# GpSimd takes the weights' remainder in two instructions of 512 columns instead of one of 1024

## The reference, cut to what matters

```python
sc = jnp.einsum('thpd,hpkd->thpk', q, subkeys)        # scores against 2 x 128 keys, 8 heads
s1, i1 = lax.top_k(sc[:, :, 0], 16)
s2, i2 = lax.top_k(sc[:, :, 1], 16)
cand = (s1[..., :, None] + s2[..., None, :])...       # 16 x 16 sums
best, pos = lax.top_k(cand, 16)                       # the experts of each token and head
gate = jax.nn.softmax(best)
act = gelu(einsum('phkd,pd->phk', u_tab[idx], t)) * gate
out = einsum('phk,phkd->pd', act, v_tab[idx])
```

## Time and profile before

| | |
|---|---|
| time, median of 3 runs | 3680.57 us (3678.1 to 3683.18) |
| the profiled execution's own time | 3682.65 us |
| its span, first to last instruction | 3680.8 us |
| TensorE busy | 3566.2 us, 97% |
| VectorE, ScalarE, GpSimd busy | 2295.2, 1473.8, 960.2 us |
| GpSimd's 63 subtractions (L289) | 167.9 us |
| mean granted TensorE clock | 0.989 |

### The profile page before, as it was taken

One profiled execution on the slowest core, in us unless ns is written; L12 is line 12 of the kernel. 1 busy time (PEld: TensorE's weight loads), 2 busy tenths in 40 slices (PEclk: granted clock), 3 DMA queues, 4 the chain that ended last, 5 costly groups with the idle time before them and its releaser, 6 DMA issues. The chain is left out here.

```text
span 3680.8 us, 55968 instructions
## 1 busy us (share of the span) xinstructions
PE 3566.2 (97%) x22572; PEld 3258.7 (89%) x22572; DVE 2295.2 (62%) x3902; ACT 1473.8 (40%) x2191; POOL 960.2 (26%) x795
## 2 busy tenths in 40 slices
PE   8999999999999998999999999999999999999998
PEld 8988999998887688888668876899999999999998
DVE  7445465545754546555686444469988886677775
ACT  7254453223635435222475433333333443333333
POOL 4010022112401013111114000058956662111110
PEclk9999999999999999999999999999999999999999
DMA  4211233222221133222221222347869999999884
GB/s 153 70 46 59 75 115 98 92 92 86 70 70 58 52 109 120 93 97 92 80 79 49 75 93 75 96 150 260 258 197 262 294 285 338 314 308 309 306 308 137
DMA packets 293616, 544.69 MB, mean 148 GB/s; under 512 B 138288, under 2 KB 187568, under 8 KB 292976
## 3 DMA queue, kind: packets, MB, share of 16 engines
q1 hardware_dynamic: 185248, 394.34, 32.7%
q0 software_dynamic: 27648, 100.68, 8.2%
q10 hardware_dynamic: 80464, 46.10, 4.2%
HBM read 483.67 MB, written 56.62 MB: 147 GB/s over the span
## 5 line engine op out<-in xcount | busy, mean ns | idle before, releaser
L314 PE MATMUL PSM<-UX,PARTS 128*128 128x264 f32 (+3 forms) x2976 | 1017.0, 342 | 33.5 <-POOL PARTS L289 6.8
L272 ACT ACTIVATE PARTS<-RAW 128x1024 fp32r<-128x1024 f32 x612 | 645.3, 1056 | 953.0 <-PE PSM L316 486.8
L315 PE MATMUL PSM<-UX,PARTS 128*128 128x264 f32 (+3 forms) x2976 | 1001.3, 336 | 0.0
L316 PE MATMUL PSM<-UX,PARTS 128*128 128x264 f32 (+3 forms) x2976 | 1000.2, 336 | 0.0
L282 DVE TENSOR_TENSOR PARTS<-RAW,PARTS 128x1024 fp32r<-128x1024 f32 x549 | 694.2, 1270 | 487.8 <-ACT PARTS L272 487.6
L314 PEld LDWEIGHTS PSM<-UX,PARTS 128*128 128x128 f32 x2976 | 562.6, 189 | 91.0 <-issue 15.7
L315 PEld LDWEIGHTS PSM<-UX,PARTS 128*128 128x128 f32 x2976 | 562.5, 189 | 35.3 <-issue 1.9
L316 PEld LDWEIGHTS PSM<-UX,PARTS 128*128 128x128 f32 x2976 | 561.4, 189 | 35.0
L3102 PE MATMUL PSM<-AC,PARTS 128*128 128x416 f32 x1024 | 359.9, 351 | 2.2 <-DVE AC L3399 2.2
L3103 PE MATMUL PSM<-AC,PARTS 128*128 128x416 f32 x1024 | 359.1, 351 | 0.0
L3104 PE MATMUL PSM<-AC,PARTS 128*128 128x416 f32 x1024 | 359.1, 351 | 0.0
(11 more groups left out here) (510 smaller groups left out, 5858.6 us busy)
## 6 DMA issues: line engine op xcount, KB each, us to landing
RAW<-w_ff_dram SPq DMA_DIRECT2D x128, 512.0 KB, 3.2
RAW<-peer_u_dram SPq DMA_DIRECT2D x128, 512.0 KB, 4.4
RAW<-peer_v_dram SPq DMA_DIRECT2D x128, 512.0 KB, 5.1
RAW<-w_in_dram SPq DMA_DIRECT2D x116, 512.0 KB, 3.3
acts_dram<-MQ ACTq DMA_DIRECT2D x128, 208.0 KB, 4.4
MQ<-acts_dram SPq DMA_DIRECT2D x128, 208.0 KB, 3.9
MQ<-gates_dram SPq DMA_DIRECT2D x128, 208.0 KB, 4.8
RAW<-w_mix_o_dram SPq DMA_DIRECT2D x32, 512.0 KB, 3.5
```

The costliest lines, as they stand in the source:

```text
L272: e.activation(p[:, 0:1024], self.raw.of(i), ACT.Copy).then_inc(S.sem, S.tick("w", i))
L314: e.matmul(dst, wh[k], xh_[k][:, lo:hi], start=(k == 0), stop=False, skip_group_check=True)
L315: e.matmul(dst, wh[k], xl_[k][:, lo:hi], start=False, stop=False, skip_group_check=True)
L316: m = e.matmul(dst, wl[k], xh_[k][:, lo:hi], start=False, stop=(k == kk - 1), skip_group_check=True)
```

## The change

The one subtraction of 1024 columns becomes two of 512 columns, one behind the other in GpSimd's program, on the left and the right half of the same block. Only the second reports its end to the others, so TensorE, VectorE and the load of the next RAW buffer wait as before for the whole block. Nothing else is touched, and 63 instructions more are issued on GpSimd.

```diff
             def pool(self, e, i):
-                p = self.parts.of(i)
+                p, r = self.parts.of(i), self.raw.of(i)
                 e.wait_ge(S.sem, S.at("w", i))
-                e.tensor_tensor(p[:, 1024:2048], self.raw.of(i), p[:, 0:1024].bitcast(F), SUB).then_inc(
-                    G.sem, G.tick("w", i))
+                for lo in (0, 512):
+                    m = e.tensor_tensor(p[:, 1024 + lo:1536 + lo], r[:, lo:lo + 512], p[:, lo:lo + 512].bitcast(F), SUB)
+                m.then_inc(G.sem, G.tick("w", i))
                 self.raw.give(G, i)
```

## The result

| | before | after |
|---|---|---|
| median of 13 runs each | 3683.05 us (3677.19 to 3687.01) | 3691.05 us (3684.9 to 3694.42) |
| the profiled execution | 3682.65 us, span 3680.8 | 3692.12 us, span 3690.0 |

The ratio is 1.0022, with a 95% interval of 1.0015 to 1.0029. The change costs 8.1 us (5.5 to 10.7). I had predicted 3682, with a range up to 3690, so the prediction was too low, and the time lies outside the range. The prediction counted from a median of 3680.57, and the kernel before had 3683.05 in the set compared here. Set against each other as changes, 8.1 us were measured where 1.5 had been forecast, and the upper end of the range stood for 9.4 (3690 less 3680.57). So the size of the forecast failed by 6.6 us, and that the time itself lies 1 us outside the range is owed to the 2.5 us between the two medians of before.

What follows compares the result with a forecast made beforehand. TensorE is bound by its work, losing only 12.6 us to waits for GpSimd and VectorE; GpSimd's 9.6 less 4.2 leaves 5.4 us, of which +1.5 reaches the end: 3682 in terms of the median, range 3675 to 3690.

Steps and rivals of the forecast that it cites:

- The seam: Point between GpSimd's two half subtractions: taken as open, so that a waiting VectorE operation goes first there.
- The extra instruction: GpSimd's subtraction: both halves take 2.54 us against 2.41, 0.13 more, 63 times, 8.2 us of GpSimd's time.
- The ordinary block with an open seam: GpSimd's loop outside heavy stretches: dot ends at 2.39, second half at 3.54, gather 0.95; 4.67 us, 0.32 more than before.
- what the lead gives back: Heavy stretches and 128x256 casts: VectorE, a block ahead, spares GpSimd waits for the dot; 4.2 us regained.
- the port: Turn only one of GpSimd and VectorE has where their operations meet; each dot costs GpSimd 1.10 us of it.
- the sum on GpSimd: Thirty ordinary blocks at 0.32 each, 9.6 us, less 4.2 regained: the last subtraction ends about 5.4 us later.
- What of it reaches the end: Before the gates: VectorE's one-hots stay last; delay 5.4 less lead 5.8 gives -0.4, late meetings up to +3; taken +1.5 us.
- The clock: TensorE's clock drops behind longer waits: three such waits before and after, so nothing counted.
- Rival A: Seam shut: 0.13 us in each of 42 blocks, loop 4.48, VectorE tied to GpSimd, gates 5.5 us later, 3686.1; chance 0.22.
- Rival B: Faster: rows land earlier, dot begins during the gather, loop 4.37, gates up to 6 us earlier, 3673; chance 0.14.
- Rival C: Slower: each handing over at the seam costs dispatch time x; with 0.4 it is 11.7 us, 3692; chance 0.12.

## Why the prediction was wrong, point by point

**The seam.** This is the step that failed: "I take the seam as open". In ordinary blocks it is shut., on which I relied, have no gather ahead of the two instructions. The earlier trace rows had one, and they showed the very case: subtractions right behind a gather, and a dot that wasn't let in. I put them aside as "something of its own". The kernel after repeats them at 2484 us, with four halves:

```profile
2483.11 0.94 POOL L3437 DMA_INDIRECT MQ<-peer_rows_dram,MQ  x1 [0.30 <-issue]
2484.07 5.05 POOL L290 TENSOR_TENSOR PARTS<-RAW,PARTS 128x512 fp32r<-128x512 f32 x4
...
2483.80 6.42 DVE L3356 SCALAR_TENSOR_TENSOR MQ<-MQ 128x1024 f32<-128x1024 f32 x1
```

The dot waited through all four, three seams. That the seam is shut in ordinary blocks is shown by the timelines, and that the cause lies ahead of the pair by the kernel that waits there.

What shuts it is not shown. The rows show that an instruction of GpSimd's can start before the one ahead is over: behind a gather the small write takes 0.12 us, and the subtraction starts 0.05 us after the write's start. That such an overlap keeps the seam shut was my guess, and no trace shows it. What the runs show is where the seam was shut and where it was open. With halves it was shut directly behind a gather (22 of 22). It was open behind a wait for GpSimd's own last instruction (25 of 25), in a row of halves that began after an idle stretch (5 of 5), and behind a gather where the first half was held (2 of 2). The quarters do not fit this, since they let VectorE in behind a gather in 11 of 13 cases.

**The extra instruction.** Right. The halves take 1.29 to 1.31 us and the pair 2.54 to 2.56, where 2.54 was predicted, with the rounded format too.

**The ordinary block with an open seam, and what the lead gives back.** The forecast counts 1.10 us "of the port" for each dot. No run shows a port. The runs show that a dot ends 1.09 us behind the half that it waited for in the kernel after, and 1.10 us in the one with the wait at the seam. Neither the open block nor the lead came about in the kernel after: gathers stayed at 1.76 and VectorE stayed tied to GpSimd. With the seam opened by a wait, both did, to 0.01 us in the block shown (3.55, 0.96 and 4.68). The last subtraction came 5.2 us later, where the sum on GpSimd said 5.4. The stage cost 2.98 us where the forecast said 1.5, so VectorE's lead gave back 2.2 us of GpSimd's lateness and not 3.9. That kernel's median, 3687.1, lies within the range. The sum was sound in the main, for a seam that isn't there.

**What of it reaches the end.** The sentence "a TensorE that is late by 5.4 still finds the one-hots the last to come" was right, but of no use: the one-hots are as late as TensorE. The wait before the gates is 4.79 before and 4.81 after. VectorE loses each tenth that GpSimd loses, since its dot has to wait out both halves. The clock was put down for nothing, with three drops before and after. There were three before and four after, 6.8 us more at 0.50, and TensorE's busy time rose by 3.3 us. Up to the gates none of that shows beside GpSimd's lateness. How much of the 0.7 us between the stage's 7.39 and the 8.1 of the runs comes from the drop at the gates, the scatter does not let one say.

**Rival A** happened, at a chance of 0.22. It gave a loop of 4.48 (4.49 measured) and 5.5 us. That is what the ordinary blocks cost (5.6). It left out the heavy stretches, 1.76 us, where the seam, shut elsewhere, is open and lets in L3306. That is the rest of the 7.39.

**Rival B** needed an open seam. **Rival C** had the right size for the wrong reason: with the wait at the seam the pair took 3.55 us, so handing over costs nothing that can be seen.

## What to carry to other kernels

Splitting an instruction lets another engine in at the seam only if the seam is free: with halves none of 22 requests got in directly behind a gather, and all of 25 behind a wait. On GpSimd look at what stands directly ahead of the pair (a gather or an idle stretch) and at whether its first instruction is held. When a row contradicts the mechanism that a forecast rests on, make it a case with its own sum rather than set it aside. Where two engines hold each other in a closed loop and both are nearly full (GpSimd 91 to 92% and VectorE 99% busy here), price time added to each block on one as time on both: 0.14 us in each of 40 blocks made 5.6 us of the stage, and TensorE's later wait, 4.79 us before and 4.81 after, absorbed none of it. A wait that looks like loss can be what keeps one engine from being held by the other (without the wait for the dot the stage took 18.07 us longer), so price its removal on the engine that would be held instead.

## What the runs showed of the hardware that I had not expected

- Directly behind a gather, two GpSimd instructions of 512 columns in a row did not let VectorE in between them (22 of 22 requests). In a row of halves that began after an idle stretch (5 of 5) or behind a wait for GpSimd's own last instruction (25 of 25) VectorE got in at the seam, and also behind a gather where the first of the two had itself been held (2 of 2).
- A write of one column takes 0.10 to 0.12 us on GpSimd, but right behind a gather it delayed the next instruction by only 0.05 us.
- The stage took 346.84, 346.95 and 346.86 us in executions of three kernels whose stage hardly differs, while whole executions scattered by some 10 us (3677.19 to 3687.01). One figure for the stage told apart changes (1.28 us for the write ahead of the subtraction) that 10 runs of the whole barely did.
